# Norms of all tiles inside the last expert's round of a three-block transformer kernel

## What is computed

```python
def expert_choice_moe(x, w_router, w_gate_up, w_down):        # cap = 128
    gates, idx = lax.top_k(jnp.swapaxes(aff, 1, 2), cap)
    xs = x[bi, idx]
    g, u = jnp.split(jnp.einsum('becd,edf->becf', xs, w_gate_up), 2, axis=-1)
    out = jnp.einsum('becf,efd->becd', jax.nn.silu(g) * u, w_down) * gates[..., None]
    return jnp.zeros_like(x).at[bi, idx].add(out)

for layer in range(2):
    mix = windowed_gqa_sink(x, ...) if layer == 0 else bidir_rglru_block(x, ...)
    x = layer_norm(ALPHA * x + mix, ln_mix_g[layer], ln_mix_b[layer])
    ffn = expert_choice_moe(x, ...)
    x = layer_norm(ALPHA * x + ffn, ln_ffn_g[layer], ln_ffn_b[layer])
```

## Time and profile before

| | |
|---|---|
| median of 3 runs | 4663.47 us (4659.9 to 4665.36) |
| the profiled execution, its own time | 4664.44 us |
| its span, first to last instruction | 4662.6 us |
| PE busy | 4198.5 us (90%) |
| DVE, ACT, POOL busy | 1576.8, 1067.1, 266.8 us |
| granted PE clock, mean over the span | 0.953 |
| DMA | 798.8 MB, 171 GB/s |

### The profile page before, as it was taken

The page is one execution under the profiler, slowest core; times in us unless marked ns, Lnnn a source line. Parts: engine busy times, 40 slices in busy tenths (PEclk is TensorE's granted clock), DMA queues, the critical chain, the costliest instruction groups (busy, mean ns, idle before and its releaser), DMA issues. The chain is left out here.

```text
span 4662.6 us, 61269 instructions
## 1 busy us (share of the span) xinstructions
PE 4198.5 (90%) x23090; PEld 2180.6 (47%) x23091; DVE 1576.8 (34%) x2934; ACT 1067.1 (23%) x1827; POOL 266.8 (6%) x304
## 2 busy tenths in 40 slices
PE   8999996788999889969899599999699995999995
PEld 5554435775444444434455244444344452444442
DVE  4554554443302422223565410111256444011002
ACT  1354223443100011111453100000246331000002
POOL 0000002221000010010000000000000000000000
PEclk9999998999999899989899799999799997999998
DMA  2301244333212399951104588888411244888894
GB/s 82 144 10 45 63 161 124 75 83 107 70 29 86 110 358 358 358 207 42 42 20 167 172 320 315 311 318 315 155 45 32 71 157 167 314 314 316 314 315 164
DMA packets 408236, 798.83 MB, mean 171 GB/s; under 512 B 140384, under 2 KB 274400, under 8 KB 375136
## 3 DMA queue, kind: packets, MB, share of 16 engines
q1 hardware_dynamic: 377920, 694.41, 42.5%
q0 software_dynamic: 16704, 60.82, 4.5%
q10 hardware_dynamic: 13408, 40.70, 2.2%
HBM read 678.41 MB, written 117.44 MB: 171 GB/s over the span
## 5 line engine op out<-in xcount | busy, mean ns | idle before, releaser
L2887 PE MATMUL ec0e_pg<-ec_wg,ec0e_xT 128*128 128x512 f32 x1024 | 444.2, 594 | 2.1 <-DVE ec0e_xT L2941 2.1
L2887 PE MATMUL ec1e_pg<-ec_wg,ec1e_xT 128*128 128x512 f32 x1024 | 443.9, 594 | 2.1 <-DVE ec1e_xT L2941 2.1
L2887 PEld LDWEIGHTS ec0e_pg<-ec_wg,ec0e_xT 128*128 128x128 f32 x1024 | 195.3, 191 | 248.2 <-issue 248.2
L2887 PEld LDWEIGHTS ec1e_pg<-ec_wg,ec1e_xT 128*128 128x128 f32 x1024 | 195.1, 191 | 248.0 <-issue 248.0
L1405 PE MATMUL mix_pb<-h_h_all,mix_wg 128*128 128x512 f32 x512 | 224.2, 597 | 9.5 <-DMA mix_wg<-in_w_in_dram 9.5
L2914 PE MATMUL ec0e_py<-gqa_wd,ec0e_hidT 128*128 128x512 f32 x512 | 226.2, 595 | 2.8 <-ACT ec0e_hidT L2932 2.8
L2914 PE MATMUL ec1e_py<-lru_wd,ec1e_hidT 128*128 128x512 f32 x512 | 226.2, 595 | 2.8 <-ACT ec1e_hidT L2932 2.8
L3172 PE MATMUL lrui_pA<-lrui_xT,lrui_w 128*128 128x512 f32 x512 | 224.1, 597 | 2.6 <-ACT lrui_xT L3246 2.6
L699 PE MATMUL front_pz<-h_h_all,front_w 128*128 128x512 f32 x480 | 211.5, 598 | 8.3 <-DMA front_ones<-in_head_ones_dram 8.3
L2949 DVE TENSOR_TENSOR ec0e_hid<-ec0e_sg,ec0e_pg 128x512 f32<-128x512 f32 x32 | 22.0, 687 | 426.2 <-ACT ec0e_sg L2929 426.2
L2949 DVE TENSOR_TENSOR ec1e_hid<-ec1e_sg,ec1e_pg 128x512 f32<-128x512 f32 x32 | 22.0, 687 | 426.0 <-ACT ec1e_sg L2929 426.0
(11 more groups left out here) (551 smaller groups left out, 6240.7 us busy)
## 6 DMA issues: line engine op xcount, KB each, us to landing
ec_wg<-in_moe_w_gate_up_dram SPq DMA_DIRECT2D x256, 1024.0 KB, 6.6
gqa_wd<-in_moe_w_down_dram SPq DMA_DIRECT2D x128, 512.0 KB, 4.5
lru_wd<-in_moe_w_down_dram SPq DMA_DIRECT2D x128, 512.0 KB, 4.5
moe_wb<-in_w_dram SPq DMA_DIRECT2D x32, 1024.0 KB, 12.3
...
```

The source lines that it names most:

```text
L2887: return nc.tensor.matmul(pg[:, b, :], xT[:, k, :], wg[:, k, b * HALF:(b + 1) * HALF], start=k == 0, stop=k == KD - 1)
```

## The change

The tiles' LayerNorm moves into the last expert's round. When the scatter of expert 14 has landed, `acc` is final except for the 128 rows of expert 15. So SP loads all 8 tiles then, and they are normed beside expert 15, whose round is written out behind a loop of 15. The normed tiles go to DRAM, with the wrong values in 128 rows. Those rows are treated alone: POOL gathers them from `acc` into `rows` (and in layer 0 into `old`, which is normed as a ninth tile), DVE adds py x gate, and expert 15 isn't scattered any more. `norm_phase` and the norm at the head of `lru_mix` go. A new `Layers` object holds what lives over both layers: `ident`, the tiles (`aT`), `wd`, `gb`, `rows`, `old`, `place`, `small`. The seventeenth gather and its transposes go too.

On SP, in `choice_phase` (`end` is true in layer 1; the gain and bias loads `gb`, in layer 1 only before, are now in both):

```diff
+if not end:
+    sp.dma_start(place[:, :], steps.partition_broadcast(P)).then_inc(steps_in, 16)
...
+sp.wait_ge(sent, E2)
+for t in range(NT):
+    sp.dma_start(tile(t), acc_dram[t * P:(t + 1) * P, :]).then_inc(tile_in[t], 16)
+for t in range(NT):
+    sp.wait_ge(o_ready, t + 1)
+    sp.dma_start(out_dram[t * P:(t + 1) * P, :], tile(t)).then_inc(tile_out, 16)
```

On POOL, behind the loop:

```diff
+nc.gpsimd.tensor_copy(at_last[:, :], idx[:, LAST:LAST + 1]).then_inc(at_ready, 1)
...
+gather(1)
+pool.wait_ge(y_ready, E2)
+pool.indirect_dma_start(acc_dram, bass.IndirectOffsetOnAxis(ap=ic[0][:, :], axis=0), y[:, :], None, compute_op=ALU.add).then_inc(added, 16)
+pool.wait_ge(added, 16 * LAST)
+pool.sem_inc(sent, 1)
+pool.indirect_dma_start(rows[:, :], None, acc_dram, bass.IndirectOffsetOnAxis(ap=at_last[:, :], axis=0)).then_inc(rows_in, 16)
+if not end:
+    pool.indirect_dma_start(old[:, :], None, acc_dram, bass.IndirectOffsetOnAxis(ap=at_last[:, :], axis=0)).then_inc(old_in, 16)
+pool.wait_ge(x_in, 16 * E2)
+if end:
+    pool.wait_ge(fix_ready, 1)
+    pool.wait_ge(tile_out, NO)
+    pool.indirect_dma_start(out_dram, bass.IndirectOffsetOnAxis(ap=at_last[:, :], axis=0), fixed[:, :], None).then_inc(fix_out, 16)
+    pool.wait_ge(fix_out, 16)
```

On ACT, with `LAST` = 15, `FIRST` = 3, `MIDDLE` = 4 and `ALL` = 9 tiles in layer 0, 8 in layer 1 (a last square and root for `rows` in layer 1 are not shown):

```diff
+def stats(t):
+    if t < NT:
+        act.wait_ge(tile_in[t], 16)
+    else:
+        act.wait_ge(old_in, 16)
+    if t:
+        act.wait_ge(sum_done, t)
+    nc.scalar.activation(junk[:, :], tile(t), ACT.Copy, accum_out=small[:, t, 0:1]).then_inc(sum_done, 1)
+    act.wait_ge(nm_ready, t + 1)
+    if t:
+        act.wait_ge(sq_done, t)
+    else:
+        act.wait_ge(x_psum, E2 + 1)
+    nc.scalar.activation(xg[:, :], tile(t), ACT.Square, bias=small[:, t, 1:2], accum_out=small[:, t, 2:3]).then_inc(sq_done, 1)
...
+top(LAST)
+for t in range(FIRST):
+    stats(t)
+silu_half(LAST, 0)
+for t in range(FIRST, MIDDLE):
+    stats(t)
+silu_half(LAST, 1)
+keep_hid(LAST)
+for t in range(MIDDLE):
+    roots(t)
+for t in range(MIDDLE, ALL):
+    stats(t)
+    roots(t)
```

On DVE (`R` is the slot of the 128 rows):

```diff
+def norm(t, other=None):
+    dve.wait_ge(sum_done, t + 1)
+    mean(t, t)
+    if other is not None:
+        scaled(other)
+    mean_squares(t, t)
+    centred(tile(t), tile(t), t)
...
+if not end:
+    nc.vector.tensor_copy(small[:, R, 6:7], idx[:, LAST:LAST + 1]).then_inc(at_f, 1)
+    dve.wait_ge(at_f, 1)
+    dve.wait_ge(steps_in, 16)
+    nc.vector.tensor_scalar(place[:, :], place[:, :], small[:, R, 6:7], None, ALU.is_equal)
...
+for t in range(FIRST):
+    norm(t)
+gated(LAST, 0)
+for t in range(FIRST, MIDDLE):
+    norm(t)
+gated(LAST, 1)
+keep_hid(LAST)
+for t in range(MIDDLE, ALL):
+    norm(t, t - MIDDLE)
+dve.wait_ge(rows_in, 16)
+dve.wait_ge(d_used, now(LAST, KD, KD))
+nc.vector.scalar_tensor_tensor(rows[:, :], py[:, :], gate[:, LAST:LAST + 1], rows[:, :], ALU.mult, ALU.add,
+                               accum_out=small[:, R, 0:1]).then_inc(rows_ready, 1)
+rest = range(ALL - MIDDLE, ALL)
+if end:
+    dve.wait_ge(rows_ready, 1)
+    mean(ALL, R)
+    dve.wait_ge(nm_ready, ALL + 1)
+    centred(fixed[:, :], rows[:, :], R)
+    mean_squares(ALL, R)
+    scaled(rest[0])
+    dve.wait_ge(root, ALL + 1)
+    V.link(nc.vector.reciprocal(small[:, R, 5:6], small[:, R, 4:5]))
+    nc.vector.scalar_tensor_tensor(fixed[:, :], fixed[:, :], small[:, R, 5:6], gb[:, 1, :], ALU.mult, ALU.add).then_inc(fix_ready, 1)
+    rest = rest[1:]
+for t in rest:
+    scaled(t)
```

In `lru_mix` PE transposes the normed tiles straight from SBUF. They hold the old values of the 128 rows; `change` is new minus old, and `place` is 1 where a token is the row's, so that `change` x `place`, 16 matmuls, corrects `xT`:

```diff
+def changed(k):
+    if k >= 2:
+        pe.wait_ge(xT_ready, k - 1)
+    for h in range(2):
+        m = nc.tensor.matmul(pA[:, 2 * (k % 2) + h, :], change[:, k * P:(k + 1) * P], place[:, halves[h]], start=True, stop=True)
+    m.then_inc(c_psum, 1)
...
-for t in range(4):
+for t in range(NT):
     turn(t)
-branch(0, 0)
-turn(4)
-turn(5)
-branch(1, 0)
-turn(6)
-turn(7)
-branch(0, 1)
-branch(1, 1)
+pe.wait_ge(change_ready, 1)
+for k in range(KD):
+    changed(k)
+for i in range(2):
+    branch(i, 0)
+    branch(i, 1)
```

DVE makes the rows and adds the corrections, and POOL writes the rows to DRAM:

```diff
+def fixed_rows():
+    nc.vector.tensor_scalar(small[:, R, 1:2], small[:, R, 0:1], -1.0 / D, None, ALU.mult).then_inc(nm_ready, 1)
+    dve.wait_ge(nm_ready, 1)
+    V.link(nc.vector.scalar_tensor_tensor(fixed[:, :], rows[:, :], small[:, R, 1:2], gb[:, 0, :], ALU.add, ALU.mult))
+    dve.wait_ge(sq_done, 1)
+    nc.vector.tensor_scalar(small[:, R, 3:4], small[:, R, 2:3], 1.0 / D, LN_EPS, ALU.mult, ALU.add).then_inc(ms_ready, 1)
+    dve.wait_ge(root, 1)
+    V.link(nc.vector.reciprocal(small[:, R, 5:6], small[:, R, 4:5]))
+    nc.vector.scalar_tensor_tensor(fixed[:, :], fixed[:, :], small[:, R, 5:6], gb[:, 1, :], ALU.mult, ALU.add).then_inc(fix_ready, 1)
+    dve.wait_ge(fix_ready, 1)
+    nc.vector.tensor_tensor(change[:, :], fixed[:, :], old[:, :], ALU.subtract).then_inc(change_ready, 1)
...
+    dve.wait_ge(c_psum, k + 1)
+    b = 2 * (k % 2)
+    nc.vector.tensor_tensor(xT[:, k, :], xT[:, k, :], pA[:, b:b + 2, :].rearrange("p a t -> p (a t)"), ALU.add).then_inc(xT_ready, 1)
...
+pool.wait_ge(fix_ready, 1)
+pool.wait_ge(layers.tile_out, 16 * NT)
+pool.indirect_dma_start(x_dram, bass.IndirectOffsetOnAxis(ap=layers.at[:, :], axis=0), fixed[:, :], None).then_inc(fix_out, 16)
+pool.wait_ge(fix_out, 16)
```

More of the change, by code:

```diff
@@ L2793, in _, with choice_phase, tile @@
             nc.vector.tensor_copy(gate[:, :], pl[:, E2:2 * E2])
-def choice_phase(nc, name, ident, x_dram, acc_dram, gate, idx, weights, ln_ffn=None, gb=None, gb_in=None):
+def choice_phase(nc, name, layers, x_dram, acc_dram, gate, idx, weights, ln_ffn, out_dram, steps, end):
+    LAST, R, FIRST, MIDDLE = E2 - 1, NT + 1, 3, 4
+    ident, tiles, gb, rows, old, place, small, at_last = (layers.ident, layers.aT, layers.gb, layers.rows, layers.old, layers.place, layers.small,
+                                                          layers.at)
+    gb_in, tile_out = layers.gb_in, layers.tile_out
+    NG = 32 * (2 if end else 1)
+    NO = 16 * NT * (2 if end else 1)
+    ALL = NT if end else NT + 1
+    def tile(t):
+        return tiles[:, t, :] if t < NT else old[:, :]
     with Phase(nc, name) as ph:
@@ L2871, in _, with one_expert @@
                 turn_x()
-                with pe.Fori(0, E2) as e:
+                def one_expert(e, more):
                     def turn_hid(half):
```

329 lines of the change are left out of this document (135 added, 194 removed).

## The result

| | before | after |
|---|---|---|
| median | 4661.7 us (4656.5 to 4665.4) | 4621.4 us (4616.4 to 4624.3) |
| span of the profiled execution | 4662.6 us | 4618.2 us |
| PE busy | 4198.5 us (90%) | 4204.2 us (91%) |
| from the first output product of layer 0 (`ec0p`) to the end | 2229.4 us | 2188.8 us |

A second comparison gave 4624.3 beside 4659.8 us, ratio 0.9921 (0.9908 to 0.9935), 35.5 us. The medians can't settle 5 us. The last line of the table can. I call it the **stretch**: in front of it stands code that the change doesn't touch, which ends 5 to 6 us earlier or later in two executions of one kernel, while the stretch repeats within 1.0 us before and 0.3 us after.

What follows compares the result with a forecast made beforehand. TensorE was taken as busy for nearly all of the span except two holes, one after each layer's last expert. 15.0 + 22.9 - 2.4 - 0.3 = 35.2 us off the profiled 4664.4 gave 4629 us, range 4622 to 4644.

Steps and rivals of the forecast that it cites:

- Part 2: LRU block's start: transposes, then 16 correction matmuls, put the projections at 3363.4; gain 15.0 us, at worst 8.6.
- Part 1: Tile norms inside the last expert's round: cost 0 with 3.3 us to spare; LRU block begins at 3336.5.
- rival (a): LRU block's start: the transposes don't lift the clock, 6.4 us of the gain go, 4635; chance 0.12.
- The bound of 15.1 for the best case: LRU block's start: largest gain allowed in the best-case sum of 38.5 us (4625).
- a ring through both engines: Tail of the tile norms: each tile's steps pass through ScalarE and VectorE in turn, 3.1 us a tile.
- From the gate products on ... the gain is kept: LRU block after its projections: queues unchanged and TensorE the limit, so the 15.0 us gain stays whole.
- Part 3: End of layer 1: last norms, stores and the rows' scatter end at 4639.7 instead of 4662.6; gain 22.9 us (19.3 to 25).
- Part 4: Added cost: loads beside layer 0's first gather 2.4 us (1.6 to 3.2), leaving the expert loop 0.3 (0 to 4.6).
- 19.3: End of layer 1: lower bound of the 22.9 us gain, used in the worst-case sum of 20 us (4644).
- the worst case of Part 2: LRU block's start: projections begin at 3369.8 at worst, leaving a gain of 8.6 us.

Runs made afterwards that it cites:

- e3_first4: Changed kernel with four instead of three tiles' sums and squares ahead of the last expert's first Silu half, the fifth between halves: stretch 2186.1 us, ratio 0.9907.
- e7_early_roots: Changed kernel with the roots of tiles 0 to 2 ahead of the first Silu half and their scale passes earlier on VectorE: stretch 2178.0 us, ratio 0.9900.
- e8: Changed kernel with gain, bias and place loads later, roots and their passes early, tile 4's norm ahead of the hidden copy: stretch 2177.8 us, ratio 0.9881.
- e12: Changed kernel with five instead of three tiles' sums and squares ahead of the first Silu half, the sixth between the halves: stretch 2197.0 us.
- e2_after: Changed kernel run again as it is, for a second profiled execution and a narrower ratio: stretch 2189.1 us, ratio 0.9921.
- e4: Changed kernel with gain, bias and place loads ahead of the last expert's loads, not beside the first gather: stretch 2183.3 us, ratio 0.9903.
- e1: Kernel before, run again as it is for a second profiled execution: stretch 2230.4 us.
- e6: Kernel before with only layer 1's last expert round written as in the changed kernel: stretch 2203.9 us, ratio 0.9958.
- e5: Changed kernel without the 16 correction matmuls and VectorE's eight additions, for measurement only: stretch 2179.9 us.

## Why the forecast came out 5 us short

The two large terms were right in kind: both holes shrank by what was moved out of them. Two things in the sum failed, the size of Part 2 and a term that stood at nothing, the clock behind the LRU block's waits.

**Part 1's cost of nothing** held: the third tile's square ended 4.1 us ahead of the first Silu (3.3 forecast), and the 0.82 us that TensorE waits in the last round stand in the place of the transposes that went.

**Part 2, the LRU block's start**, is the term that was mis-sized. Forecast 15.0 us; measured, from layer 0's last product to the gate products, 99.4 - 80.9 = 18.5. The block began 13.95 us behind that product, not 15.9: the last mean of squares came 1.0 us sooner (3324.14, on before's scale 3324.4: the first of the five was 0.6 us early, and the ring ran at 2.99 us, not 3.1), the passes 0.4, and three exits took 1.9 us and not 2.5 with the store. The turns took 10.3 us (10.8 forecast; rival (a) is refuted by the 2.01 us rows), the corrections with all waits 15.3 (16.1), and the projections' 41.28 us from start to gates stood as 41.7. Each was small and all had one sign. The bound of 15.1 for the best case was no bound: I had put spread on the clock alone. The mechanism that I gave for the tail was off too, though it cost little here: a ring through both engines, where VectorE's passes set the time (e3_first4, e7_early_roots).

**"From the gate products on ... the gain is kept"** is the step that failed. 3.6 us more came there, out of code that the change doesn't touch: 3.2 because before's clock fell behind two waits (8.61 and 8.83 us for 16 records) and after's didn't (7.13 both), 0.4 because the second wait was 3.23 us and not 3.62. The corrections' removal shows the other sign, 5.8 us lost. This term had no place in my sum or my range. That it came out as a gain is the luck of this kernel: e3, e8 and e12 begin the block in the same way and paid it once or twice. In "middle" 1.4 us went the other way, and there too the clock differs: the first 48 records behind a wait of 5.0 us took 23.83 us in after and 22.54 in before.

**Part 3, the end**: 22.9 forecast, 23.6 to 23.9 measured. The stores' issue ended 12.2 us behind the last product (13.3 forecast), the scatter's issue 3.4 us later and the end 8.8 behind that (8.4). Inside the 8.4 both parts were wrong and nearly cancelled, which is luck. The view of the DMA issues of the last 18 us of after (tensors, queue, count, us from issue to landing):

```profile
out_dram<-ec1e_fixed,layers_at POOLq DMA_INDIRECT x1, 3.3
```

The plain indirect write lands after 3.3 us, not 6.0, and 5.5 us then pass to the end, where I had 2.4. The Trainium skill (DMA: Bandwidth & Descriptors, Anatomy of one DMA — SWDGE (gpsimd) path) gives 3.2 us by estimate for these 512 KB. This row agrees; the accumulating scatter's 6.6 us don't. Nor does the same plain write of layer 0, which goes to DRAM beside the LRU block's weight loads (DMA issues of e2_after):

```profile
x<-lrui_fixed,layers_at POOLq DMA_INDIRECT x1, 7.4
```

The accumulating scatters show the same: in before they land 8.8 to 9.8 us after issue in the first 14 rounds of a layer, while weights are loading, and 6.0 to 6.3 in the last two, after the last weights. So the 6.6 us of expert 14 are the price without weight loads beside it, and Part 1 could use them, since that scatter stands there in the changed kernel too: 6.5 and 6.7 us to landing in e2_after.

**Part 4**: 2.7 us forecast; experts 0 is 3.5 us longer in the first pair of profiles and 3.1 in the second. The gather's wait, 9.5 and 9.7 us beside 6.4 in before, is 3.2 of that, the upper bound of my range. Leaving the loop costs nothing that shows.

Sum by the cuts: 18.5 + 3.6 - 1.4 - 3.5 - 0.2 + 23.6 = 40.6 us, the difference of the first two stretches. The medians of the second comparison, 35.5 us apart, would have met the forecast; the stretch, which leaves the code ahead of it out, says that this would have been luck. Two bounds weren't what my own terms give: 22.9 - 0.6 - 2.3 is 20.0 and not 19.3, and the worst case of Part 2 left the 0.8 us of waits out. Neither touched the end of the range that was missed.

**What stays open** is what decides whether the clock falls behind a wait of 3.24 us. Behind the first of the two waits, the same length and the same code, 16 records took 7.13 (after, twice; e4, e7), 8.6 to 8.8 (before, e1, e3, e6, e8, e12) or 9.95 us (e5). Before and after, the two kernels that were profiled twice, repeated their own. That wait began 238.6 to 238.8 us behind the block's first transpose where the clock stood (after, e4, e7) and 238.4 to 238.5 where it fell (e3, e6, e8, e12). Behind the second wait, 16 records took 7.13 us where it began at 271.07 (e3) and over 10 where it began at 271.16 (e8, e12). So a few tenths of a us seem to be enough. But in before and e1 the first wait began at 239.4 and 239.6 and the clock fell too, so it isn't that distance alone; I have no rule for it.
